# Two heads' value products together, in alternating halves of the output's partitions

## The reference, cut to what matters

```
s = (q @ k.T) * 96 ** -0.5            # 256 x 256, causal mask added
p = softmax(s)
o = p @ v                              # 256 x 64 a head, 16 heads side by side
y_mla = o @ w_mla_out                  # 1024 -> 1024
```

## Time and profile before

| | |
|---|---|
| median of 3 runs | 1355.56 us (1354.67 to 1355.86) |
| the profiled execution | 1355.45 us, its span 1353.6 us |
| TensorE, products busy | 1302.0 us, 96% of the span |
| TensorE, loads busy | 1204.5 us, 89% |
| VectorE busy | 1029.9 us, 76% |
| ScalarE busy | 871.2 us, 64% |
| GpSimd busy | 90.0 us, 7% |
| mean granted clock | 0.992 |

### The profile page before, as it was taken

How to read it: one execution, slowest core, us unless ns; L and a number is a source line. 1 busy time by engine, 2 the same in 40 slices (tenths; PEclk the granted TensorE clock), 3 DMA queues, 4 the chain that set the end, 5 groups by cost and what they waited for, 6 DMA issues and landing times.

```text
span 1353.6 us, 23806 instructions
## 1 busy us (share of the span) xinstructions
PE 1302.0 (96%) x9401; PEld 1204.5 (89%) x9405; DVE 1029.9 (76%) x1535; ACT 871.2 (64%) x1289; POOL 90.0 (7%) x81
## 2 busy tenths in 40 slices
PE   7999999999999999999999899999999999999993
PEld 7989999998999998999999888999987777788882
DVE  6676655567655558998998886775469999999994
ACT  6565444456444556676555766555458999999993
POOL 0000100001000000000001200110000221111113
PEclk9999999999999999999999999999999999999997
DMA  8643555553555543654534624454365999999963
GB/s 274 203 152 127 190 185 184 186 184 115 187 186 186 186 148 119 193 172 141 164 121 134 244 94 156 161 183 156 107 245 211 355 368 369 367 388 380 374 245 127
DMA packets 150108, 279.78 MB, mean 207 GB/s; under 512 B 13721, under 2 KB 122238, under 8 KB 136574
## 3 DMA queue, kind: packets, MB, share of 16 engines
q1 hardware_dynamic: 141952, 269.97, 57.7%
q0 software_dynamic: 7696, 8.41, 2.1%
q10 hardware_dynamic: 366, 0.12, 0.0%
HBM read 274.26 MB, written 21.50 MB: 218 GB/s over the span
## 4 chain that ended last, share of the span: by engine, by line
PE 78%; DVE 14%; issue 3%; ACT 3%; DMA 1%; DVEq 0%; POOLq 0%; POOL 0%; SPq 0%; ACTq 0%
PE psum L854 18%; PE psum L856 18%; PE psum L855 18%; PE psum L1414 3%; PE psum L1413 3%; PE psum L1415 3%; DVE weights_parts L2087 2%; DVE weights_parts L2693 2%; PE psum L1439 2%; PE psum L1440 2%; PE psum L1441 2%; DVE arena L2477 2%; DVE expert_parts L2693 1%; ACT weights_parts L1478 1%; PE psum L1258 1%
## 5 line engine op out<-in xcount | busy, mean ns | idle before, releaser
L2087 DVE TENSOR_TENSOR weights_parts<-ring,weights_parts 128x1024 fp32r<-128x1024 f32 (+3 forms) x312 | 363.3, 1184 | 161.3 <-ACT weights_parts L1478 160.9
L1478 ACT ACTIVATE weights_parts<-ring 128x1024 fp32r<-128x1024 f32 (+3 forms) x312 | 308.9, 1009 | 175.4 <-PE psum L856 175.1
L854 PE MATMUL psum<-xnorm_parts,weights_parts 128*128 128x256 f32 x884 | 255.6, 289 | 5.9 <-DVE xnorm_parts L2236 2.0
L855 PE MATMUL psum<-xnorm_parts,weights_parts 128*128 128x256 f32 x884 | 249.1, 282 | 0.0
L856 PE MATMUL psum<-xnorm_parts,weights_parts 128*128 128x256 f32 x884 | 248.9, 282 | 0.0
L854 PE MATMUL psum<-expert_cols,weights_parts 128*128 128x256 f32 (+1 forms) x688 | 194.8, 283 | 3.3 <-DVE expert_cols L2105 2.0
L856 PE MATMUL psum<-expert_cols,weights_parts 128*128 128x256 f32 (+1 forms) x688 | 192.1, 279 | 0.0
L855 PE MATMUL psum<-expert_cols,weights_parts 128*128 128x256 f32 (+1 forms) x688 | 192.1, 279 | 0.0
L854 PE MATMUL psum<-hidden_parts,weights_parts 128*128 128x256 f32 x640 | 182.0, 284 | 2.5 <-DVE hidden_parts L2545 1.7
L855 PE MATMUL psum<-hidden_parts,weights_parts 128*128 128x256 f32 x640 | 180.6, 282 | 0.0
L856 PE MATMUL psum<-hidden_parts,weights_parts 128*128 128x256 f32 x640 | 180.5, 282 | 0.0
(11 more groups left out here) (422 smaller groups left out, 2529.6 us busy)
## 6 DMA issues: line engine op xcount, KB each, us to landing
expert_raw<-in_w_exp_down SPq DMA_DIRECT2D x35, 1024.0 KB, 6.9
ring<-in_mlp_w_up SPq DMA_DIRECT2D x32, 1024.0 KB, 5.5
ring<-in_mlp_w_down SPq DMA_DIRECT2D x32, 1024.0 KB, 4.8
ring<-in_w_in SPq DMA_DIRECT2D x30, 1024.0 KB, 5.4
ring<-in_w_exp_gate SPq DMA_DIRECT2D x23, 1024.0 KB, 6.7
ring<-in_w_exp_up SPq DMA_DIRECT2D x23, 1024.0 KB, 9.1
ring<-in_attn_w_qkv SPq DMA_DIRECT2D x12, 1024.0 KB, 8.2
expert_raw<-in_w_exp_gate SPq DMA_DIRECT2D x12, 1024.0 KB, 6.6
```

What stands on the lines that cost most here:

```text
L854: pe.matmul(out, lh, rh, start=start, stop=False, **more)
L855: pe.matmul(out, lh, rl, start=False, stop=False, **more)
L1478: ins = act.activation(high, src, ACT.Copy)
L2087: ins = dve.tensor_tensor(low, src, high.bitcast(F32), ALU.subtract)
```

## The change

`attention` on TensorE no longer calls the value products in every iteration, but in the one of the group's last head, with all heads of the group and their transposed copies. `values2` then writes four products: the first of the even head (partitions 0 to 63), the first of the odd head (64 to 127), the second of the even head, the second of the odd head. For the other two attentions a group is one head, and their instructions stay where they were. The programs of VectorE, ScalarE, GpSimd and SyncE are the same instruction for instruction. After L905 line numbers differ: the scores are L1249 and L1250 in the changed kernel, the value products L1258 and L1261.

```diff
--- before.py
+++ after.py
@@ -905,13 +905,11 @@
                     if meanwhile is not None:
                         meanwhile(i)
                     n = i - at.o_lag
-                    if n >= 0:
-                        lead = at.lead(n)
-                        b = open_bank("O", lead) if n % at.pair == 0 else FILL["O", lead][0]
+                    if n >= 0 and n % at.pair == at.pair - 1:
+                        b = open_bank("O", at.lead(n))
                         wait_made("T", at.first + n)
-                        mm = values(n, b, PROB_T[at][:, n % at.t_bufs, :])
-                        if n % at.pair == at.pair - 1:
-                            mm.then_inc(full[b], 1)
+                        heads = range(n - at.pair + 1, n + 1)
+                        values(heads, b, [PROB_T[at][:, h % at.t_bufs, :] for h in heads]).then_inc(full[b], 1)
@@ -1250,15 +1249,18 @@
-            def values2(h, b, pt):
-                if h % 8 == 0:
+            def values2(heads, b, turned):
+                if heads[0] % 8 == 0:
                     for tb in range(TB):
-                        wait_made("vh", h // 8 * 2 + tb)
-                o = bank(b)[64 * (h % 2):64 * (h % 2) + 64, :]
-                pe.matmul(o[:, 0:TOK], vh[:, 0, h * VH:(h + 1) * VH], pt[:, 0:TOK], start=True, stop=False,
-                          skip_group_check=True)
-                return pe.matmul(o[:, P:TOK], vh[:, 1, h * VH:(h + 1) * VH], pt[:, TOK:TOK + P],
-                                 start=False, stop=True, skip_group_check=True)
+                        wait_made("vh", heads[0] // 8 * 2 + tb)
+                out = [bank(b)[VH * e:VH * (e + 1), :] for e in range(2)]
+                for o, h, pt in zip(out, heads, turned):
+                    pe.matmul(o[:, 0:TOK], vh[:, 0, h * VH:(h + 1) * VH], pt[:, 0:TOK], start=True, stop=False,
+                              skip_group_check=True)
+                for o, h, pt in zip(out, heads, turned):
+                    mm = pe.matmul(o[:, P:TOK], vh[:, 1, h * VH:(h + 1) * VH], pt[:, TOK:TOK + P],
+                                   start=False, stop=True, skip_group_check=True)
+                return mm
```

More of the change, by code:

```diff
@@ L996, in scores1, with values1 @@
                 return pe.matmul(bank(b)[:, P:3 * P], qk[:, h, P:TOK], qk[:, H1 + h, :], start=True, stop=True)
-            def values1(h, b, pt):
+            def values1(heads, b, turned):
+                (h,), (pt,) = heads, turned
                 wait_made("v1", h // 2)
@@ L1313, in scores3, with values3 @@
                 return mm
-            def values3(h, b, pt):
+            def values3(heads, b, turned):
+                (h,), (pt,) = heads, turned
                 wait_made("xv", h)
```

## The result

| | before | changed |
|---|---|---|
| median | 1354.74 us (1354.5 to 1355.86, 6 runs) | 1347.78 us (1347.06 to 1348.2, 6 runs) |
| profiled execution, its span | 1355.45, 1353.6 us | 1347.5, 1345.7 us |
| TensorE, products busy | 1302.0 us | 1294.9 us |
| mean granted clock | 0.992 | 0.992 |

The ratio is 0.9941, with a 95% interval of 0.9931 to 0.9951, which is 8.0 us (6.6 to 9.3); the two medians by themselves are 6.96 us apart, the two profiled executions 7.95. The forecast was 4.8 us, 1350.8, and its range ended at 6.8 us, 1348.8. The direction was right, and that the second head's products lie beside the first's was right. The size was 2 to 3 us too small, above all because VectorE was taken to hold two pairs at 9.40 us, where they take 8.79.

A forecast was written before the change was run, and what follows sets the result against it. TensorE was taken to bound the latent attention, VectorE second. Gains 0.97 + 3.48 + 0.62 - 0.30 = 4.77 us gave 1350.8 us in the median's terms; the forecast's own range was 1348.8 to 1351.5, the 8-in-10 range 1348.8 to 1354.1.

The forecast's parts named there:

- first pair: Start of the attention stage: a 1.3 us wait goes, the second transposition starts 1.2 us earlier; gain 0.97 us.
- four pairs without a root: Pairs of latent-attention iterations bound by TensorE, from 9.71 to 8.84 us each; gain 3.48 us.
- two pairs with a root: Attention pairs also holding VectorE's inverse root, bound by VectorE at 9.40 us where 9.71 before; gain 0.62 us.
- last visit: Stage's last value products: 6.73 us behind the earlier visit carried over whole, 0.15 added for each of two visits; -0.30 us.
- Part 1: Even heads' value products leave eight odd iterations of TensorE's stream, 0.99 us each, 7.9 us.
- Part 2: Eight visits hold four value products instead of two; the array's halves run side by side, adding 0.15 us a visit.
- Part 3: VectorE's rounds limit what is kept: four pairs TensorE-bound at 8.84 us, two with an inverse root VectorE-bound at 9.40.
- A: Value products' halves don't overlap in so short a group: pairs of 9.39, gain 1.4 us, 1354.1; chance 0.12.
- B: Round from scores over VectorE and ScalarE to copy binds every pair, about 9.40; gain 2.5 us, 1353.0; chance 0.12.
- C: Gain is given back behind the stage, where ScalarE and VectorE split the weights; 1355.4 us; chance 0.05.
- D: TensorE's granted clock falls after waits in the stage, 1.7 us a fall; five falls give 1359.3 us; chance 0.05.

## Why the prediction was wrong

The terms of its sum beside what the traces show:

| term | forecast | measured |
|---|---|---|
| first pair | 0.97 | 1.06 |
| four pairs without a root | 3.48 | 38.55 - 34.59 = 3.96 |
| two pairs with a root | 0.62 | (9.84 + 9.80) - (8.79 + 8.78) = 2.07 |
| last visit | -0.30 | 6.73 - 6.16 - 0.01 = 0.56 |
| sum | 4.77 | 7.65 |

(First pair: 777.72 - 777.09 = 0.63, and the stage's first output projection started 763.64 - 763.21 = 0.43 us later than in the trace before.) The two profiled executions differ by 7.95 us. The 0.43 us were lost ahead of the stage, and some 0.7 us were gained behind 1009 us, both in parts that the two kernels share; nothing here shows by what.

- **Part 1 held.** Eight visits are gone at 0.99 us each, 7.9 us, about the whole gain: a pair without a root went from 9.64 to 8.65. The 0.2 us of slower entry and exit were only a part of what the width costs in it: the same visit 128 columns wide costs 0.66 us, 0.33 less.
- **The first pair held.** The transposition's start moved from 774.46 to 773.81, 1.08 us within a stage that begins 0.43 later, where 1.2 were forecast, and its copy was not delayed by VectorE. The clock has no part in it: the stretch at the lower level only comes later with the stage, and from the first product of the output projection to the first of the next iteration it is 768.59 - 763.21 = 5.38 us before and 769.01 - 763.64 = 5.37 after.
- **Part 2, "I take 0.15 us a visit", was mis-sized: 0.01.** The sum has it six times, in four pairs and in the last two visits: 6 x 0.14 = 0.8 us. I read the lag from the earlier trace rows, where the second head's first pass came 0.27 us after the first's, with six passes ahead of it, and took a lag for a cost. (The group there has eight heads and not four, 48 passes.) In the short visit both streams are as long as each other and end together, and neither order of the products delays the second (0.80 and 0.81 us). Of the two rules of the Trainium skill that the prediction weighed (TensorE: Matmul & The Clock Gate), the about 4 ns for each further tile (Measured speedup vs the span model) agree with the 0.01 us of this trace. The strict program order (The mechanism) does not agree with the run with head after head.
- **Part 3, "the two with the root by VectorE (9.40)", is the step that failed most, by 1.45 us.** Such a pair takes 8.79 and 8.78 us, not 9.40 (1.23 us for the two), and took 9.84 and 9.80 before, not 9.71 (0.22 us). The 58.26 us behind the 9.71 are also 0.07 too long, since they run from a row of the timeline to one of the chain; by the chain alone it is 835.98 - 777.79 = 58.19. The 9.40 was a sum of durations, and VectorE's instructions overlap. The timeline of VectorE in the changed kernel, one weight piece to the one two iterations on, within which it hardly stands still:

```profile
783.84 1.22 DVE L2090 TENSOR_TENSOR weights_parts<-ring,weights_parts 128x1024 fp32r<-128x1024 f32 x1
...
785.39 1.74 DVE L2535 RECIPROCAL std<-std 128x256 f32<-128x256 f32 x1
...
787.16 0.69 DVE L2548 TENSOR_TENSOR hidden_parts<-arena,hidden_parts 128x512 fp32r<-128x512 f32 x1
787.77 0.42 DVE L2239 TENSOR_TENSOR xnorm_parts<-psum,xnorm_parts 128x256 fp32r<-128x256 f32 x1
788.11 0.55 DVE L2208 SCALAR_TENSOR_TENSOR arena<-psum,consts_sb 128x384 f32<-128x384 f32 x1
...
789.22 1.21 DVE L2090 TENSOR_TENSOR weights_parts<-ring,weights_parts 128x1024 fp32r<-128x1024 f32 x1
...
792.66 1.22 DVE L2090 TENSOR_TENSOR weights_parts<-ring,weights_parts 128x1024 fp32r<-128x1024 f32 x1
```

  The same work that adds up to 9.40 us passes in 792.66 - 783.84 = 8.82 us. The 0.42 us of L2239 are followed 0.34 later, the 0.69 of L2548 0.61 later. The rule that I stated myself for TensorE, that starts and not durations give the time in the stream, holds for VectorE too. 8.82 is hardly above TensorE's 8.65, and so a root costs 0.14 us and not 0.56. Without the roots all pairs are 8.65, and in the kernels whose pairs TensorE holds at 8.87 to 9.29 us a root adds nothing, which it would if VectorE needed 9.40.
- **The last visit was mis-sized by 0.86 us**, 0.28 of it the two times 0.14 of part 2. "The last transposition then meets probabilities that are ready only as it arrives" was right (scaled at 833.51 + 0.50 = 834.01, transposition at 834.16), but by the visit left out it comes 4.91 us behind the visit at 829.25, where it came 841.52 - 835.91 = 5.61 behind that visit before. ScalarE's weight piece took back only 0.13 of these 0.70: from transposition to visit 1.32 us against 842.71 - 841.52 = 1.19. I had carried over 6.73 us whole for want of a walk through it.
- **The rivals.** A (no overlap) is what the run with both heads in one half builds: it gains 2.5 us, where the prediction gave A 1.4, with pairs of 9.29 and not 9.39. B named a round over VectorE and ScalarE as a bound for every pair. There is such a round, and the kernel before stood at it with all but the last even head's products; it needs those products in the odd iterations, and the changed kernel has none there. C did not come (7.23 us at the stage's end, 7.21 at the experts). D did not either (granted clock 1.00 from 772 to 836 us).
- **The range.** Its lower end was 1348.8, a gain of 6.8 us, with the second half free and the roots absorbed. Both nearly came about, but that end gave the last visit no gain at all, and it brought 0.56 us, more than half of the 0.9 us between 6.8 and 7.65.

## What to carry to other kernels

Two small products that use different halves of the array's columns cost here no more than one, to within 0.02 us, when they stand in the same short group, in either order; look for products of 64 columns that a pipeline issues one head at a time. Grouping them also takes half of the meetings with the softmax away, which is worth something where a pipeline is near the latency of its round: the passes made cheaper alone saved 0.66 us a pair in the stream and brought 0.14. When a stage is priced by an engine's work, take starts to starts over a stretch without idle time, since durations overlap on VectorE as on TensorE.

## What was not expected of the hardware

- TensorE starts products out of program order across the two halves of its columns: in the run with head after head, the four passes of both first products stand ahead of the passes of the even head's second.
- A float32 product of 32 moving columns costs 0.22 us between longer ones with 128 stationary columns, and 0.42 with 64.
- VectorE's rows start about 0.08 us before the row ahead of them ends, so that 9.4 us of durations pass in 8.82.
- The same four passes of a head's value products cost 0.99 us among 128-column neighbours when they are 64 columns wide, and 0.66 when they are 128 wide.
